# Layer norm sums ahead of the last projection unit, spread attention turns, and two RMS norms with squares summed on VectorE

## What is computed

```python
def layer(x):                                    # 1024 prompt rows and 64 sample rows of 1024
    x = x + 0.5 * ffn(rmsnorm(x), ffn1)
    q, k, v, a, g = split(rmsnorm(x) @ w_in)     # 512 columns each
    A = window_attention(q, k, v)                # 8 heads, prompt and samples
    y = depthwise_conv(a * sigmoid(g)) + conv_b  # 512 channels, 31 taps
    B = silu(layernorm(y) * ln_g + ln_b)
    x = x + [A | B] @ w_out
    x = x + softmax(rmsnorm(x) @ w_cq @ mk.T / 16) @ mv @ w_co
    x = x + 0.5 * ffn(rmsnorm(x), ffn2)
    return rmsnorm(x)
# rmsnorm(x) = x * rsqrt(mean(x * x) + 1e-6) * gain
# also returned: the new key, value and conv caches and the memory's keys and values
```

## Time and profile before

| what | us |
|---|---|
| median of 3 runs | 2849.64 (2840.91 to 2853.72) |
| profiled execution, whole | 2857.73 |
| its span, first to last instruction | 2855.8 |
| TensorE busy with matmuls | 2642.7 (93%) |
| VectorE, ScalarE, GpSimd busy | 1055.2, 544.8, 694.2 |
| mean granted TensorE clock | 0.968 |

### The profile page before, as it was taken

One profiled execution on the slowest core, in us unless ns is written; L12 is line 12 of the kernel. 1 busy time (PEld: TensorE's weight loads), 2 busy tenths in 40 slices (PEclk: granted clock), 3 DMA queues, 4 the chain that ended last, 5 costly groups with the idle time before them and its releaser, 6 DMA issues.

```text
span 2855.8 us, 43744 instructions
## 1 busy us (share of the span) xinstructions
PE 2642.7 (93%) x16847; PEld 2474.4 (87%) x16847; DVE 1055.2 (37%) x1987; ACT 544.8 (19%) x1301; POOL 694.2 (24%) x404
## 2 busy tenths in 40 slices
PE   7999999999998999588798988869899999999998
PEld 6899999999997999566456888739799999999998
DVE  5133332223336797234332231631532222333334
ACT  4100000000003233365221122320300000000002
POOL 6522222222220321130001210102222222222220
PEclk9999999999999999799998999989999999999999
DMA  6311111111110121345973112661111111111101
GB/s 211 118 45 44 44 44 44 44 44 44 44 44 15 43 76 63 125 138 141 260 222 104 44 46 76 223 231 44 40 42 43 44 44 44 44 44 44 44 30 63
DMA packets 215073, 224.86 MB, mean 79 GB/s; under 512 B 11706, under 2 KB 181750, under 8 KB 210899
## 3 DMA queue, kind: packets, MB, share of 16 engines
q1 hardware_dynamic: 197943, 195.58, 22.6%
q10 hardware_dynamic: 17052, 28.21, 2.7%
HBM read 191.10 MB, written 32.67 MB: 78 GB/s over the span
## 4 chain that ended last, share of the span: by engine, by line
PE 82%; DVE 5%; DMA 5%; issue 4%; ACT 2%; PEld 1%; POOL 1%; SPq 1%; DVEq 0%; ACTq 0%; PEldq 0%; POOLq 0%
PE ps L678 24%; PE ps L680 23%; PE ps L679 23%; PE ps L1026 1%; PE ps L1070 1%; DVE hidl L1708 1%; PE ps L953 1%; PE ps L964 1%; DMA Kw<-in_cache_win_k 1%; DMA Vn<-out_new_win_v_sample 1%; PE ps L1040 1%; DVE hl L1674 1%; PE ps L936 1%; PE ps L1175 1%; PE ps L1120 1%
## 5 line engine op out<-in xcount | busy, mean ns | idle before, releaser
L678 PE MATMUL ps<-hh,wh 128*128 128x384 f32 (+1 forms) x3168 | 1040.8, 329 | 51.4 <-DVE hl L1750 26.8
L680 PE MATMUL ps<-hl,wh 128*128 128x384 f32 (+1 forms) x3168 | 1038.6, 328 | 0.0
L679 PE MATMUL ps<-hh,wl 128*128 128x384 f32 (+1 forms) x3168 | 1038.6, 328 | 0.0
L678 PEld LDWEIGHTS ps<-hh,wh 128*128 128x128 f32 x3168 | 600.0, 189 | 55.3 <-issue 51.7
L679 PEld LDWEIGHTS ps<-hh,wl 128*128 128x128 f32 x3168 | 599.9, 189 | 0.1
L680 PEld LDWEIGHTS ps<-hl,wh 128*128 128x128 f32 x3168 | 599.5, 189 | 0.0
L620 POOL CAST wh<-raw 128x1024 fp32r<-128x1024 f32 x148 | 154.8, 1046 | 1505.9 <-PE ps L680 1375.7
L1720 DVE TENSOR_TENSOR ht<-ps,sg 128x384 f32<-128x384 f32 x132 | 70.7, 536 | 927.4 <-PE ps L680 926.0
L622 POOL TENSOR_TENSOR wl<-raw,wh 128x1024 fp32r<-128x1024 f32 x148 | 365.0, 2466 | 11.9
L678 PE MATMUL ps<-hidh,bh 128*128 128x384 f32 (+1 forms) x1056 | 346.6, 328 | 11.7 <-DVE x L1732 11.7
L1732 DVE SCALAR_TENSOR_TENSOR x<-ps,x 128x384 f32<-128x384 f32 (+1 forms) x528 | 276.5, 533 | 185.3 <-PE ps L680 184.8
(11 more groups left out here) (229 smaller groups left out, 2071.3 us busy)
## 6 DMA issues: line engine op xcount, KB each, us to landing
raw<-in_ffn_gate SPq DMA_DIRECT2D x44, 512.0 KB, 3.9
raw<-in_ffn_up SPq DMA_DIRECT2D x44, 512.0 KB, 3.8
raw<-in_ffn_down SPq DMA_DIRECT2D x44, 512.0 KB, 3.5
Kw<-in_cache_win_k SPq DMA_DIRECT2D x48, 256.0 KB, 7.2
Vw<-in_cache_win_v SPq DMA_DIRECT2D x48, 256.0 KB
raw<-in_w_in SPq DMA_DIRECT2D x20, 512.0 KB, 3.7
Kw<-in_cache_win_k SPq DMA_DIRECT2D x8, 1024.0 KB, 13.7
Vw<-in_cache_win_v SPq DMA_DIRECT2D x8, 1024.0 KB
```

Of the source, the lines that this page charges most:

```text
L678: pe.matmul(out, w_hi_, a_hi, start=first, stop=False)
L679: pe.matmul(out, w_lo_, a_hi, start=False, stop=False)
L680: return pe.matmul(out, w_hi_, a_lo, start=False, stop=last)
```

## The change

Both norms behind `w_out` and `w_co` and the layer norm behind `w_in` are reordered, and with them the start of the window attention.

- Layer norm: squares go to `U` for chunks 0 and 1 and to `sq_ln` for chunk 2 (`square_home`); `ln_squares` moves one unit forward, `ln_sums` from behind the last unit to behind the one before it; roots are taken in `ln_roots` beside the last unit. Barriers 3 become arrivals. `ln_end` does SiLU and store by chunk, and stands behind the conv and key stores. `cct` moves, and its copy stands before the variances.
- Attention: in each round only `vT` of the first pair is turned at the start; `vc` and `kTp` follow in steps 0 and 1, the second pair's turns in steps 7, 8 and 9. TensorE waits for `qs` at a pair's start, and for `kc` at step 2 of a pair only.
- Norms: ScalarE squares each tile of `x` as soon as it is complete, VectorE adds the squares in `sums`, and TensorE does for each chunk two ones products, of `sums` and of the last square; that of chunk 0 stands inside the last but one tile. ScalarE takes the root straight from PSUM, with scale and eps. Scaled tiles go to banks 4 and 5. The order at the end is in `tail_order`. `w_cq` runs chunk outside, unit inside, in groups of four units, with `stage` of four buffers. Barriers 7 and 10 become arrivals.

The diff, cut:

```diff
@@ def turns(n)
-        early = {WP - 3: [("f", 1, 0), ("f", 1, 1)], WP - 2: [("v", 1, 0), ("v", 1, 1)],
-                 WP - 1: [("k", 1, 0), ("k", 1, 1)]}
+        early = {0: [("f", 0, 0), ("f", 0, 1)], 1: [("k", 0, 0), ("k", 0, 1)], WP - 1: [("v", 1, 0), ("v", 1, 1)],
+                 WP: [("f", 1, 0), ("f", 1, 1)], WP + 1: [("k", 1, 0), ("k", 1, 1)]}
...
+    def square_home(c):
+        return U[:, :, 384 * c:384 * c + 384] if c < 2 else sq_ln
+    def tail_order():
+        seq = [("add", 0, 0), ("root", 0, 0), ("inv", 0, 0), ("add", 1, 0)]
+        for c in range(NC):
+            for k in range(KT):
+                seq.append(("tile", c, k))
+                if c == 0 and k == 2:
+                    seq.append(("add", 2, 0))
+                if c < NC - 1 and k == 4:
+                    seq.append(("root", c + 1, 0))
+            if c < NC - 1:
+                seq += [("lo", c, KT - 1), ("inv", c + 1, 0)]
+        return seq
@@ TensorE
+            def row_sum(c):
+                n, j = CHUNKS[c][1], NC * (KT - 1) + c
+                pe.wait_ge(sn["var"], sn.base["var"] + NC * (KT - 3) + c + 1)
+                pe.matmul(ps[:, 5 + c, 0:n], ones[:], sums[:, c, 0:n], start=True, stop=False)
+                pe.wait_ge(sn["sq"], sn.base["sq"] + j + 1)
+                pe.matmul(ps[:, 5 + c, 0:n], ones[:], sq[:, j % 4, 0:n], start=False, stop=True
+                          ).then_inc(sn["summed"], 1)
...
+                        if k == 4 and j == NC * KT - 2:
+                            row_sum(0)
...
+            for c in range(1, NC):
+                row_sum(c)
+        def query_proj(s):
...
+                for c, (c0, n) in enumerate(CHUNKS):
+                    pe.wait_ge(s["h"], s.base["h"] + KT * (c + 1))
+                    for w in range(4):
+                        if c == 0:
+                            pe.wait_ge(w_split, i * 4 + (u0 + w + 3))
+                        pe.wait_ge(s["free"], s.base["free"] + i * (4 * NC) + (c * 4 + w + 1))
...
             if w == 1:
                 ln_mean()
-            if w == 3:
+            if w == 2:
                 ln_sums()
...
-        barrier(pe, 3)
+        arrive(pe)
+        pe.wait_ge(S["ln"]["var"], S["ln"].base["var"] + NC)
...
-            for src in (vT, kTp, vc):
-                if src is vc:
-                    pe.wait_ge(A["sorted"], i * 6 + 3)
-                for half in range(2):
-                    tokens(src, 0, half)
+            for half in range(2):
+                tokens(vT, 0, half)
...
-        proj("w_out", S["so"], 8, CHUNKS, hh, hl, lambda c: KT * (c + 1))
-        barrier(pe, 7)
-        norm(S["nx"], CHUNKS, sq)
-        proj("w_cq", S["nx"], 8, CHUNKS, hh, hl, lambda c: KT * (c + 1))
+        out_proj("w_out", S["so"], S["nx"])
+        arrive(pe)
+        query_proj(S["nx"])
@@ ScalarE
+        def out_norm(s, sn):
...
+                act.activation(dst, x[:, w, c0:c0 + n], ACT.Square).then_inc(sn["sq"], 1)
...
+            for j in range(NC * (KT - 1)):
+                square(j)
+            act.activation(rs[:, NC - 1, 383:384], eps, ACT.Sqrt)
+            for what, c, k in tail_order():
...
+                    act.activation(rs[:, c, 0:n], ps[:, 5 + c, 0:n], ACT.Sqrt, bias=eps, scale=1.0 / D
+                                   ).then_inc(sn["std"], 1)
+                elif what == "tile":
...
+                    act.copy(hh[:, k, c0:c0 + n], ps[:, 4 + j % 2, 0:n]).then_inc(sn["hi"], 1)
...
         store_units(S["nm"])
-        ln_end()
-        barrier(act, 3)
+        arrive(act)
...
         act.dma_start(win_s["v"], kvs[:, 1, :]).then_inc(A["tokst"], 16)
+        ln_end()
...
-        norm(S["nx"], CHUNKS, x, sq, rs, tb, hh)
-        store_proj("w_cq", S["nx"], stage, KT, 0, zx)
+        out_norm(S["so"], S["nx"])
...
+        store_queries(S["nx"])
@@ VectorE
+            for j in range(NC * (KT - 1)):
+                add(j)
+                if j > NC:
+                    add_square(j - 1)
+            add_square(NC * (KT - 1) - 1)
+            for what, c, k in tail_order():
...
+                elif what == "tile":
...
+                    dve.scalar_tensor_tensor(out=ps[:, 4 + j % 2, 0:n], in0=x[:, k, c0:c0 + n],
+                                             scalar=vecs[:, gain + k:gain + k + 1], in1=rs[:, c, 0:n], op0=ALU.mult,
+                                             op1=ALU.mult).then_inc(sn["t"], 1)
+                    if k >= 1:
+                        lo(j - 1)
+            lo(NC * KT - 1)
```

More of the change, by code:

```diff
@@ L354, in blocks @@
         return cuts, [(far(t) + c, P) for c in range(0, near(t), P)]
-    WT = 6 + sum(len(turns(n)) for n in range(WN))
+    WT = 2 + sum(len(turns(n)) for n in range(WN))
     def norm_order(nc_):
@@ L881, in ln_sums @@
                     pe.wait_ge(N["sq"], N.base["sq"] + c * CT + k + 1)
-                    mm = pe.matmul(ps[:, LNB[c], 0:w], ones[:], sq_ln[:, k, 0:w], start=(k == 0), stop=(k == CT - 1))
+                    mm = pe.matmul(ps[:, LNB[c], 0:w], ones[:], square_home(c)[:, k, 0:w], start=(k == 0), stop=(k == CT - 1))
                 mm.then_inc(N["summed"], 1)
@@ L1201, in _ @@
         barrier(pe, 9)
-        proj("w_co", S["sc"], 8, CHUNKS, hh, hl, lambda c: KT * (c + 1))
-        barrier(pe, 10)
-        norm(S["n2"], CHUNKS, sq)
+        out_proj("w_co", S["sc"], S["n2"])
+        arrive(pe)
         F, N2 = S["fin"], S["n2"]
@@ L1368, in store_units @@
                     tap_samples(k)
+                if u == 3 * CT - 3:
+                    ln_squares()
                 if u == 3 * CT - 2:
[L1370 to L1372 removed]
+                    ln_roots()
         def split_input(s):
@@ new lines, in store_queries @@
+        def store_queries(s):
+            with act.Fori(0, KT // 4) as i:
+                for c, (c0, n) in enumerate(CHUNKS):
+                    for w in range(4):
+                        if c == 0:
+                            act.wait_ge(s[QUEUES[w]], s.base[QUEUES[w]] + i * 16 + 16)
+                        if c < NC - 1:
+                            act.wait_ge(s["part"], s.base["part"] + i * 8 + (4 * c + w + 1))
+                        else:
+                            act.wait_ge(unit_done, i * 4 + (SLOTS + COL["w_cq"] + w + 1))
+                        act.copy(stage[:, w, c0:c0 + n], ps[:, w, 0:n]).then_inc(s["free"], 1)
+                        if c == NC - 1:
+                            act.wait_ge(s["free"], s.base["free"] + i * 12 + (4 + 4 * c + w + 1))
+                            act.dma_start(zx[bass.ds(i * (4 * P) + w * P, P), :], stage[:, w, :]
+                                          ).then_inc(s[QUEUES[w]], 16)
+            for w in range(4):
+                act.wait_ge(s[QUEUES[w]], s.base[QUEUES[w]] + 48)
@@ L1486, in _ @@
         act.dma_start(win_s["v"], kvs[:, 1, :]).then_inc(A["tokst"], 16)
+        ln_end()
+        for w in range(2):
+            act.wait_ge(S["nm"][f"st{w}"], S["nm"].base[f"st{w}"] + 8 * 3 * CT + 16)
+        arrive(act)
+        act.sem_inc(A["t_free"], 2)
+        act.sem_inc(A["kst"], 32)
         with act.Fori(0, H // 4) as i:
@@ L1518, in _ @@
             exp(0, 1)
-            act.wait_ge(C["obst"], 16 * CT)
-            for kind in "vkf":
-                for half in range(2):
-                    tokens(kind, 0, half)
+            act.wait_ge(C["obst"], 16 * NC)
+            for half in range(2):
+                tokens("v", 0, half)
             for n in range(WN):
@@ L2052, in _ @@
         barrier(dve, 6)
-        add_proj("w_out", S["so"])
-        barrier(dve, 7)
-        norm(S["nx"], CHUNKS, x, sq, rs, tb, G_X, hh, hl)
+        add_proj("w_out", S["so"], S["nx"], G_X)
         barrier(dve, 8)
@@ L2129, in _ @@
         barrier(dve, 9)
-        add_proj("w_co", S["sc"])
-        barrier(dve, 10)
-        norm(S["n2"], CHUNKS, x, sq, rs, tb, G_FFN2, hh, hl)
+        add_proj("w_co", S["sc"], S["n2"], G_FFN2)
         F, Y = S["fin"], S["ys"]
```

156 lines of the change are left out of this document (111 added, 45 removed).

## The result

The median fell from 2850.09 us (2840.91 to 2853.72) to 2831.27 us (2821.34 to 2837.55), ratio 0.9943 (95% interval 0.9923 to 0.9962). That is 18.8 us where 38 were forecast, and 2831.3 us lies outside the range of 2801 to 2829. The profiled executions differ by more (2857.73 and 2831.27 us), since that of before was a long one; the first experiment shows in which stage.

The account below looks back on a forecast made before the run. TensorE bounds the kernel; its waits at the layer norm (25.3 us) and before projections and ffn (23.0 us) were to shrink. 13.8 + 0.5 + 16.1 + 7.6 = 38.0 us off 2849.64 gave 2812 us, range 2801 to 2829.

Parts of the forecast that it names:

- part 1: Layer norm between `w_in` and window attention: attention starts earlier, gain 13.8 us (10 to 15.5), plus 0.5 us for spreading turns.
- Then VectorE works alone: Behind `w_out`, after the first reciprocal: additions and pairs of scaled tile and `hl` make chunk 0 whole at 1636.5.
- ScalarE's own order is late next: Layer norm's end: SiLUs and stores stand behind conv and key stores, so the last store is issued at 1191.7.
- Two k turns come one step later and cost 1.5 us: Start of window attention, one step behind the first `PT` copy: two `k` turns add 1.5 us.
- rival B: Attention start: transfers hold it; with the last store landing in 11 us, part 1 gains 7 us, 2818 us; chance 0.08.
- Part 2 behind w_out: Norm behind `w_out` through `w_cq`: `w_cq` begins at 1636.5 instead of 1650.37; gain 16.1 us, bounds 12 and 19.
- The price of a pair ... is in the first norm: Norms behind projections: a pair with its tile in PSUM takes 1.11 us for 384 columns, an estimated 0.99 for 320.
- Part 2 behind w_co: Norm behind `w_co` into `ffn2`: earlier start, partly given back before the third pair; gain 7.6 us, bounds 4 and 10.
- Rival A: Norms behind projections: casts set the pace, each tail 7.4 us longer; gain 23 us, 2827 us; chance 0.15.
- C: Rival, both tails: no second stop, 3 to 4 us better each; about 47 us gained, 2803 us; chance 0.08.
- E: Rival, norms: row sum or squares hold the additions up, norms gain nothing; 14 us, 2836 us; chance 0.06.
- D: Rival, straight code of `w_out` and `w_co`: instruction supply stops, 6.1 us each; 2856 us at seven; chance 0.03.

Follow-up runs that it names:

- the first experiment: The kernel before, unchanged, run and profiled a second time against the kernel before: ratio 1.0008 (0.9989 to 1.0026).

## Why the prediction was wrong, point by point

**What bounds the kernel** was right: both places were stretches of TensorE standing still, and what was gained was gained there. Of the 38.0 us forecast 19.0 are missing by distances: 6.3 in part 1, 4.2 behind `w_out` and 8.5 behind `w_co`. The largest single step that failed is `Then VectorE works alone`, 6.9 us.

**Part 1, 14.3 us forecast, 8.0 measured** (mean of three profiles of the old order, 1340.6, and three of the new, 1332.6). Transposes directly behind the last projection unit and the variances beside it: right. `ScalarE's own order is late next`: half right. The last store of `ya` was issued at 1193.7 against 1191.7: the table load began at 1185.2 instead of 1184 (`ks` was turned only at 1181.4), and the SiLUs of 384 columns took 0.53 us each, with 0.5 us of idle per chunk, where 5.2 us for all twelve were estimated. It landed after 5.2 us instead of 4.5. Together 2.7 us: the first copy into `PT` came at 1203.5, 12.7 us earlier than before, where 13 to 15 were to show the forecast right. The failed step is `Two k turns come one step later and cost 1.5 us`: they cost 3.7. The clock was still low (granted 0.50 over the turns) and their copies stand between steps; no variant tests these two apart. 2.7 + 2.2 = 4.9 us of the 6.3. And rival B, given 0.08, was hidden right behind the forecast: with ScalarE's order mended, transfers held the start where it was. The forecast's `only one such transfer is behind` priced the transfers for a late issue only. The 0.5 us for the spreading itself is not to be seen (the second round takes 60.4 us before and 60.8 after).

**Part 2 behind w_out, 16.1 us forecast, 11.9 measured** (mean of three profiles of the old order, 224.2, and three of the new, 212.3). Squares and additions beside the projection at nothing: right. The row sum, the root and the reciprocal came nearly as forecast: the first reciprocal ended 96.5 us behind the start of `w_out`, where 95.9 were forecast. Then `w_cq` began 109.2 us behind `w_out` instead of 106.0, and the fifth tile 131.9 instead of 127.7. The failed step is `Then VectorE works alone`: GpSimd was splitting the last unit, 1.9 us. With it failed `The price of a pair ... is in the first norm`: 1.22 us, not 1.11, for three times eight pairs, about 2.5 us by the last cast. Where the 0.11 comes from stays open: the first norm has two banks too, but its scaling stands behind one wait in the program and the new one behind three, and no run tests that. The second stop came as described, 3.8 us (2.2 to 3.6 forecast), and the clock behind it was granted at 0.54 over 6 us where I had taken 3 us at the lower level; in the second profile of this kernel it was 0.76 over 6 us, so this part differs from one execution to the next.

**Part 2 behind w_co, 7.6 us forecast, -0.9 measured** (934.6 to 935.5). The same two terms: 5.0 us for three units under way instead of one, and 0.9 us of pitch, put the start 112.6 us behind that of `w_co` instead of 107.1; the third pair came at 137.4 instead of 130.6. The description of what is late next was right (the product behind the last cast), so nothing hid the 6.8 us: they came 1:1 out of a gain of 7.6. What was left went to the clock: granted at 0.58 over the 6 us behind the stop it cost 2.5 us, where 1.5 were forecast. The third pair itself did start earlier, 137.4 against 139.4 us in three profiles of the old order, but those had no stop ahead of it.

The additions of squares, too, took up to 2.68 us beside a split (0.55 alone), but they had 3.6 us of room, as forecast. So the same stall was free in one place and cost 6.9 us in another; I had looked up GpSimd for its weight slots only, not for what its instructions do to the one engine on the path. The Trainium skill (SBUF — State Buffer, SBUF: two separate sides) has the rule that I did not weigh: a VectorE instruction with two inputs in SBUF and a GpSimd instruction that reads SBUF hold a shared pair of ports exclusively, and the second to start waits for the whole of the first. These traces agree, in the ends of the long scalings (0.42 us behind GpSimd's) and in the variant with one operand in PSUM. What it describes cost 6.9 us of this forecast, and the earlier trace rows, whose scalings read `ps`, could not show it.

By the other page of the Trainium skill that the prediction drew on (ScalarE: Activation LUTs, What ACT_TABLE_LOAD costs), two loads would have cost 2.8 us more. Here the load of `ffn2` took 1.28 us, the SiLU followed at once (0.49 us) and the product came 1.91 us after the load's start, as before: the row was right to go by.

**The sum** was made from the right places: 8.0 + 11.9 - 0.9 = 19.0 us by distances, 18.8 by the medians. Rival A (15 us lost in the tails) had about the right size, 12.7, by another cause than its casts. C and E did not come true. Nor did D: in the straight code of `w_out` and `w_co` TensorE is busy 50.00 of 50 us and 60.00 of 60, and the stop of 6.13 us that D took as its price belongs to a loop's jump, for it went with the loop. (D's sum is 1.5 us too high: seven such stops against a gain of 38 give 2854.5 us.)

## What to carry to other kernels

When a change makes an engine work alone on the path, list what every other engine does in those microseconds, and check for each operand whether it lies where both reach: here one operand moved to PSUM, a third buffer, and the first copies and product put into gaps were worth 23 us (C 8.6, E 14.3), more than the whole change had brought. Compare profiles by distances between marks, and know the spread of each distance from two profiles of one kernel before giving a gain to a cause. A transfer's landing time holds only for the traffic that was on the queues when it was measured; where its issue is moved forward, it is moved into another crowd.

## What was not expected of the hardware

- A VectorE scaling with both tensors in SBUF stretched from 0.62 to as much as 2.02 us, and an addition from 0.55 to 2.68 us, beside GpSimd's splits (1.04 and 2.35 us); beside the scalings the split stretched by 0.2 us. With one operand of the scaling in PSUM neither scaling nor split did; the addition was not tried so.
- TensorE stood 4.7 to 6.6 us at a loop's jump back (a round of some 800 matmuls of other sizes) and 0 us in the same code written out.
- The granted clock behind a stop is not told by the stop's length alone. Before the fifth `w_cq` tile, behind stops of 3.0 to 4.1 us, it was 0.54 to 0.76 over the next 6 us in seven profiles; before the third pair of `ffn2`, behind stops of 4.0 us, 0.55 to 0.73 in six, and behind stops of 0.88, 2.45 and 2.65 us it stayed at 1.00. In the kernel before, a stop of 2.91 us in `w_cq` (before its second chunk) was enough for 0.52 over the next 3 us.
- Part of the spread between executions is the clock at the start of a projection. In the eleven profiles with the new order it was granted at 0.51 to 0.76 over the first 6 us of `w_out`, and the first reciprocal ended 97.2 to 95.8 us behind that start.
- The sample attention took 174.3 to 190.5 us in fourteen profiles with the same work: most of the spread of the whole kernel. Whether an earlier start makes it longer (mean 180.5 us in three profiles with the old start, 184.3 in eleven with an earlier one) can't be told from these.
